# Two weight blocks at a time behind the normed tiles, and weight buffers released in halves, in a five-layer f32 kernel

## What is computed

```python
def rms_norm(x, g):
    xf = x.astype(jnp.float32)
    y = xf * lax.rsqrt(jnp.mean(xf * xf, axis=-1, keepdims=True) + EPS)
    return (y * g.astype(jnp.float32)).astype(x.dtype)
...
        idx_logits = jnp.einsum('bqhd,bsd->bqhs', qib.astype(jnp.float32), kf) * (IDX_HEAD_DIM ** -0.5)
        score = jnp.einsum('bqh,bqhs->bqs', wib.astype(jnp.float32) * (IDX_HEADS ** -0.5),
                           jax.nn.relu(idx_logits))
        adm = chunk_id[:, None, :] <= cqb[:, :, None]
        score = jnp.where(adm, score, -jnp.inf)
        top_val, top_idx = lax.top_k(score, k_sel)
```

## Time and profile before

| | |
|---|---|
| median of 3 runs | 1811.8 us (1811.22 to 1815.78) |
| profiled execution | 1814.44 us, of it the span 1812.4 us |
| mean granted clock of PE | 0.984 of full speed |
| PE, DVE, POOL, ACT busy | 95%, 69%, 45%, 44% of the span |
| matmuls | 13216 |
| HBM read | 150.5 MB, 84 GB/s over the span |

### The profile page before, as it was taken

How to read it: one execution, slowest core, us unless ns; L and a number is a source line. 1 busy time by engine, 2 the same in 40 slices (tenths; PEclk the granted TensorE clock), 3 DMA queues, 4 the chain that set the end, 5 groups by cost and what they waited for, 6 DMA issues and landing times.

```text
span 1812.4 us, 32762 instructions
## 1 busy us (share of the span) xinstructions
PE 1720.8 (95%) x13216; PEld 1285.5 (71%) x13216; DVE 1255.6 (69%) x2284; ACT 806.4 (44%) x1501; POOL 819.5 (45%) x721
## 2 busy tenths in 40 slices
PE   5999999999998989999999999899999999999997
PEld 5677777777776768667766666587677777777766
DVE  7599999999998676369975665545688517245553
ACT  3444534435433452465434443434576533344442
POOL 3544434444433255387851111444555555544433
PEclk9999999999999999999999999999999999999988
DMA  7222221222222132222221111132222232343312
GB/s 296 93 69 74 95 87 66 85 95 72 71 95 83 59 122 94 70 70 82 82 70 35 36 35 35 39 101 84 91 71 84 70 105 80 128 128 111 108 51 92
DMA packets 51877, 154.73 MB, mean 85 GB/s; under 512 B 5888, under 2 KB 12032, under 8 KB 51600
## 3 DMA queue, kind: packets, MB, share of 16 engines
q1 hardware_dynamic: 51728, 152.65, 25.1%
HBM read 150.50 MB, written 2.13 MB: 84 GB/s over the span
## 4 chain that ended last, share of the span: by engine, by line
PE 45%; DVE 11%; ACT 4%; issue 1%; POOL 1%; DVEq 0%; ACTq 0%; POOLq 0%
PE bank L509 10%; PE bank L505 10%; PE bank L506 10%; PE bank L2266 3%; PE bank L2254 3%; PE bank L2288 2%; DVE lru_xc L2708 2%; DVE score L2378 2%; DVE best L2375 2%; PE bank L2921 1%; PE bank L2936 1%; PE bank L548 1%; PE bank L550 1%; PE bank L549 1%; PE bank L2220 1%
## 5 line engine op out<-in xcount | busy, mean ns | idle before, releaser
L487 POOL TENSOR_TENSOR w_lo<-raw,w_hi 128x512 fp32r<-128x512 f32 (+2 forms) x434 | 582.7, 1363 | 651.5 <-ACT w_hi L469 651.1
L505 PE MATMUL bank<-h_hi,w_hi 128*128 128x512 f32 x1368 | 587.0, 429 | 24.4 <-ACT h_hi L949 10.2
L509 PE MATMUL bank<-h_lo,w_hi 128*128 128x512 f32 x1368 | 544.8, 398 | 10.1 <-DVE h_lo L923 5.7
L506 PE MATMUL bank<-h_hi,w_lo 128*128 128x512 f32 x1368 | 541.5, 396 | 0.0
L469 ACT ACTIVATE w_hi<-raw 128x512 fp32r<-128x512 f32 (+2 forms) x434 | 241.9, 601 | 279.8 <-PE bank L509 196.7
L505 PEld LDWEIGHTS bank<-h_hi,w_hi 128*128 128x128 f32 x1368 | 261.1, 191 | 113.0 <-issue 53.7
L509 PEld LDWEIGHTS bank<-h_lo,w_hi 128*128 128x128 f32 x1368 | 260.5, 190 | 79.9 <-DVE h_lo L923 10.5
L506 PEld LDWEIGHTS bank<-h_hi,w_lo 128*128 128x128 f32 x1368 | 261.9, 191 | 60.2 <-issue 13.9
L1553 DVE SCALAR_TENSOR_TENSOR ya<-padded,vecs,ya 128x512 f32<-128x512 f32 x240 | 216.3, 901 | 3.9
L2323 ACT ACTIVATE probs<-probs,small 128x512 f32<-128x512 f32 x64 | 46.3, 724 | 108.9 <-DVE small L2306 108.5
L2990 DVE CUSTOM_DVE_ANT_0 fox_probs<-bank,fox_keybias 128x128 f32<-128x128 f32 (+3 forms) x64 | 28.8, 488 | 85.0 <-PE bank L2921 84.7
(11 more groups left out here) (397 smaller groups left out, 2799.8 us busy)
## 6 DMA issues: line engine op xcount, KB each, us to landing
raw<-even_in SPq DMA_DIRECT2D x57, 512.0 KB, 3.8
raw<-odd_in SPq DMA_DIRECT2D x39, 512.0 KB, 3.4
raw<-ada SPq DMA_DIRECT2D x32, 512.0 KB, 4.1
raw<-fox_in SPq DMA_DIRECT2D x25, 512.0 KB, 3.6
raw<-lru_in SPq DMA_DIRECT2D x24, 512.0 KB, 3.4
ada_first<-ada SPq DMA_DIRECT2D x16, 512.0 KB, 14.0
raw<-even_out SPq DMA_DIRECT2D x16, 512.0 KB, 3.5
raw<-odd_out SPq DMA_DIRECT2D x16, 512.0 KB, 3.4
```

What stands on the lines that cost most here:

```text
L487: e.tensor_tensor(k.w_lo[s % NSPLIT][:, at], k.raw[n % NRAW][:, at], k.w_hi[s % NSPLIT][:, at].bitcast(F32), ALU.subtract).then_inc(*did(" ...
L505: e.matmul(out, hi[:, w], x[i][0], start=start and i == 0, stop=False, skip_group_check=True)
L506: e.matmul(out, lo[:, w], x[i][0], start=False, stop=False, skip_group_check=True)
L509: m = e.matmul(out, hi[:, w], x[i][1], start=False, stop=stop and i == kt - 1, skip_group_check=True)
```

## The change

1. `half_block`, `round_half`, `rest_half`, `project`, `project_values`: projecting a block now signals twice, after step 4 and after step 8, and the first half of block n+2 may be rounded after the first signal, if it fits in the first half of n.
2. Third layer: ki and qi0 are projected alternately, a step of each; what follows on ki moves to 1.9 (`main_end`), and the wi transposes from 1.0 to 1.7 behind qi0's number. DVE scales wi behind qi0's product instead of ahead of it.
3. Fourth layer: the steps of the first pair (lru 0 and gate 8) are mixed; `recurrence_times(0)` starts at 1.3 instead of 1.0, ACT's copy at 0.72, DVE's convolution at 0.77.
4. Fifth layer: fox_f's steps are put between value steps, and ACT rounds the next block ahead of the softplus.

```diff
@@ half_block
-    return n, key, slice(half * size, (half + 1) * size), k.plan[k.split[s - NSPLIT]][0] if s >= NSPLIT else None
+    old = None
+    if s >= NSPLIT:
+        old_key, _, old_kt, old_width, _ = k.plan[k.split[s - NSPLIT]]
+        soon = half == 0 and size <= old_kt // 2 * old_width
+        old = ("projected", old_key, old_kt // 2 - 1) if soon else ("projected", old_key)
+    return n, key, slice(half * size, (half + 1) * size), old
@@ project
         if i == kt - 1:
             m.then_inc(*did("projected", key))
+        elif i == kt // 2 - 1:
+            m.then_inc(*did("projected", key, i))
@@ main_times, main_end (third layer)
+    if key in INDEX[:2]:
+        return [block_number(INDEX[0]) + (2 * i + 0.5 + INDEX.index(key)) / DT for i in range(DT)]
     return [block_number(key) + (i + 0.5) / DT for i in range(DT)]
+def main_end(key):
+    return block_number(key) + (1.9 if key == INDEX[0] else 0.99)
@@ odd, PE
     def index_weights():
-        yield block_number(("qi", 0)) + 1.0
+        yield block_number(("qi", 0)) + 1.7
...
-    merge(main(), index_weights(), turn_values(), scores())
+    merge(main(INDEX[:1]), main(INDEX[1:] + MAIN), index_weights(), turn_values(), scores())
@@ odd, DVE; the same main_end on ACT and POOL
-            at = block_number(key) + 0.99
+            at = main_end(key)
...
-                if key == ("qi", 0):
+                if key == ("qi", 1):
                     ready(("multiplied", "wi_t"))
@@ lru
-    return spread_out(recurrence_labels(), n + 1.0, n + 1.9) if n + 1 < LT else spread_out(recurrence_labels(), 0.0, 1.6)
+    return spread_out(recurrence_labels(), n + (1.0 if n else 1.3), n + 1.9) if n + 1 < LT else spread_out(recurrence_labels(), 0.0, 1.6)
...
+        at = lru_times(0)
+        return (block(("lru", 0), ("activated", "lru_in", 0), [at[i] for i in (0, 2, 3, 5, 6, 8, 9, 11)]),
+                block(("lru", LT), ("made", "lru_gate", 0), [at[i] for i in (1, 4, 7, 10, 12, 13, 14, 15)]))
...
-            yield n + 0.55
+            yield n + (0.55 if n else 0.77)
...
-            yield n + 0.5
+            yield n + (0.5 if n else 0.72)
@@ fox
-    merge(block(("fox_f", 0), ("made", "fox_f"), [0.0] * DT))
...
+    merge(values(), block(("fox_f", 0), ("made", "fox_f"), [0.5, 1.5, 2.5, 3.1, 3.2, 3.3, 3.4, 3.5]))
...
+    round_ahead(k, e, need, did, k.nth["fox_f", 0] + NSPLIT)
     exp_of_minus_abs(e, need, did, "fox_softplus", k.rows[:, 0, :], k.rows[:, 1, :], ("made", "fox_f"))
-    round_ahead(k, e, need, did, k.nth["fox_f", 0] + NSPLIT)
```

More of the change, by code:

```diff
@@ L466, in round_half @@
     n, key, at, old = half_block(k, s, half)
-    for w in need((f"raw{n % NRAW}", key), old and ("projected", old)):
+    for w in need((f"raw{n % NRAW}", key), old):
         e.wait_ge(*w)
@@ L484, in rest_half @@
     n, key, at, old = half_block(k, s, half)
-    for w in need(("rounded", key, half), old and ("projected", old), (f"raw{n % NRAW}", key)):
+    for w in need(("rounded", key, half), old, (f"raw{n % NRAW}", key)):
         e.wait_ge(*w)
@@ L531, in project_tokens, with project_values @@
     m.then_inc(*did("projected", key))
-def project_values(k, e, need, did, name, part, taken, x_ready):
+def project_values(k, e, need, did, name, part, taken, x_ready, start):
     for b in range(TT):
@@ L545, in project_values @@
                 at = slice(tt * P, (tt + 1) * P)
+                yield start + ch * TT + tt
                 for v in need(("rest_made", key, i), ("rounded", key, i), *free, *x_ready(ch)):
@@ L550, in project_values @@
                 m = e.matmul(bank[:, :], k.H[ch][1][:, at], hi[:, w], start=False, stop=ch == DT - 1, skip_group_check=True)
-        m.then_inc(*did("projected", key))
+            m.then_inc(*(did("projected", key) if i == kt - 1 else did("projected", key, i)))
 def start_gpsimd(k, e):
@@ L2221, in scores, with main @@
                      skip_group_check=True).then_inc(*did("multiplied", "score", i))
-    def main():
-        for key in INDEX + MAIN:
+    def main(keys):
+        for key in keys:
             at = main_times(key)
@@ L2548, in main @@
         for key in INDEX + MAIN:
-            yield block_number(key) + 0.99
+            yield main_end(key)
             if key[0] in ("v", "g"):
@@ L2658, in blocks @@
     def blocks():
-        for n in range(LT):
+        for n in range(1, LT):
             at = lru_times(n)
@@ L2662, in blocks, with first_blocks @@
             yield from block(("lru", LT + n), ("made", "lru_gate", n), at[DT:])
+    def first_blocks():
+        at = lru_times(0)
+        return (block(("lru", 0), ("activated", "lru_in", 0), [at[i] for i in (0, 2, 3, 5, 6, 8, 9, 11)]),
+                block(("lru", LT), ("made", "lru_gate", 0), [at[i] for i in (1, 4, 7, 10, 12, 13, 14, 15)]))
     def recurrence(n):
@@ L2673, in recurrence @@
                      skip_group_check=True).then_inc(*did("multiplied", "lru_gates", n, i))
-    merge(blocks(), chain(*(recurrence(n) for n in range(LT - 1))))
+    merge(*first_blocks(), blocks(), chain(*(recurrence(n) for n in range(LT - 1))))
     k.end("tensor", "lru")
@@ L2901, in projections, with values @@
             yield from block((name, p), ("made" if name == "fox_g" else "activated", name, p), fox_times(name, p))
-    merge(block(("fox_f", 0), ("made", "fox_f"), [0.0] * DT))
-    for part in range(2):
-        taken = [k.work.take(value_done(part, tt)) for tt in range(TT)]
-        for tt, (bank, _) in enumerate(taken):
-            k.bank["fox_v", part, tt] = bank
-        project_values(k, e, need, did, "fox_v", part, taken, h)
+    def values():
+        for part in range(2):
+            taken = [k.work.take(value_done(part, tt)) for tt in range(TT)]
+            for tt, (bank, _) in enumerate(taken):
+                k.bank["fox_v", part, tt] = bank
+            yield from project_values(k, e, need, did, "fox_v", part, taken, h, part * DT * TT)
+    merge(values(), block(("fox_f", 0), ("made", "fox_f"), [0.5, 1.5, 2.5, 3.1, 3.2, 3.3, 3.4, 3.5]))
     merge(projections(0, 2))
```

## The result

| | before | changed |
|---|---|---|
| median | 1811.22 us (5 runs, 1808.49 to 1815.78) | 1819.96 us (5 runs, 1819.48 to 1821.64) |
| profiled execution, its span | 1814.44, 1812.4 us | 1819.48, 1817.8 us |
| ratio | | 1.0047, 95% interval 1.0031 to 1.0063 |

The changed kernel is slower by 8.5 us (0.0047 x 1811.2), between 5.6 and 11.4. The forecast was 1815.5, +3.7, in a range up to 1821.0: the side on which the sum came out was right and the range holds the time, but the size was less than half. The slower rival's 1818.9 is nearer to the 1820.0 measured than the forecast is. Profiled execution against profiled execution the difference is +5.0 us, nearer to the forecast, because that of before (1814.44) was one of its slower runs.

What follows compares the result with a forecast made beforehand. TensorE, busy 95% of the span, was taken as the bound, with a four-engine chain where the change reorders. Third layer +6.9, fourth -2.7, fifth -0.5, halves 0 gave +3.7 us on the median 1811.8: 1815.5, range 1807.5 to 1821.0.

Steps and rivals of the forecast that it cites:

- slower rival: Third layer: clock falls behind all three new holes, two more low stretches of 1.7 us; +7.1 us, 1818.9; chance 0.22.
- Step A: Third layer, ki and qi0 in pairs: the pair ends at 769.3 instead of 772.13, 2.8 us won; ki ends 2.1 later.
- Step B: Third layer, ahead of qi1: a new 4 us TensorE hole turns the 2.8 us won into a loss of 0.8.
- Step C: Third layer: transposes behind six steps of qi1 (4.1 us); swaps of qi0 and first score matmul 5.2 us late.
- low end: Third layer: TensorE's later idle time takes back at most 2.9 of the 5.2 us, leaving +2.3.
- Step D: Third layer: one low-clock stretch behind the first hole delays the transposes; +1.7 us, from none to three stretches (+5.1).
- Step E: Fourth layer: four more lru1 steps fill the 2.94 us idle ahead of the gates; -2.7 us, from -4.2 to -1.2.
- Step F: Fifth layer: value steps between fox_f's fill a 0.19 us wait and two short weight-load waits; -0.5 us, -1 to -0.2.
- step G: Halves, rounding half a block earlier: ScalarE's 196.7 us of waits mostly stay; 0 us, from -1 to +0.5.
- sign of being wrong: Halves: ScalarE's 196.7 us of waits cut by a third together with TensorE's idle time would break the claim of 0.

Runs made afterwards that it cites:

- e6: Changed kernel with the wi transposes ahead of qi1 again (1.7 back to 1.0), ki and qi0 still in pairs; 1.0004 of the kernel before.
- e9: Kernel before with only the wi transposes, and VectorE's scaling of wi, moved behind six steps of qi1, no pairing; 1.0020 of before.
- e7: Changed kernel with 18 spare matmuls, results unused, in the third layer's first hole, ahead of qi1; 1.0035 of the kernel before.
- e8: e7 with 12 more spare matmuls in the second hole, ahead of qi2; 1.0032 of the kernel before.
- e4: Kernel before with the halves alone: a weight buffer's first half given back after step 4, every order as before; 1.0001 of before.
- e10: e5 with 14 spare matmuls in the fourth layer's hole ahead of lru1; 0.9980 of the kernel before.
- e1: Kernel before with the third layer's part alone: ki and qi0 in pairs, wi transposes behind six steps of qi1; 1.0046 of before.
- e2: Kernel before with the fourth layer's part alone: the first pair's steps mixed, its recurrence placed later; 0.9986 of before.
- e5: Changed kernel with the third layer's part taken back; 0.9988 of the kernel before.
- e11: e6 with 14 spare matmuls in the hole ahead of the early transposes; 1.0008 of the kernel before.
- e3: Kernel before with the fifth layer's part alone: fox_f's steps between value steps, rounding ahead of the softplus; 1.0000 of before.

## Why the prediction was right in its side and short in its size

The forecast was +3.7 us with 0.60 on a change too small to be measured and 0.28 on a slower kernel; it is slower, clear of its interval. The mechanism of the loss was named, hole by hole. The time lies within the range because the range's top was drawn from the slower rival, and only one of that rival's two further low stretches is the change's doing. So the range held in part by luck.

**Step A** (2.8 us won at the pair's end). Measured 2.1: qi0 ends 13.1 us in instead of 15.2. The term took eight slow spacings from the start, and there were eleven and a shorter twelfth (the full pace is back at 762.33, 5.2 us in, not 3.6).

**Step B** (qi1 0.8 us later). The mechanism was right, down to POOL's w_lo as the releaser and a hole of 4.13 us where 4 were expected. qi1 starts 17.7 us in instead of 15.9, so 1.8 late where the term had 0.8. Of that 1.0 us, 0.8 comes from A's error: the last matmul of ki is 12.5 us in (769.62), not 11.7. The other 0.2 is the relay from there to qi1, 5.2 us instead of 5.0: POOL's w_lo follows ScalarE's rounding by 0.97 us (772.54 to 773.51), not by half a rounding, and the last leg is shorter. With the transposes put back, the pairing still costs 2.2 us to the first score (e6). This term was less than half of what it should have been.

**Step C** (transposes behind six steps, 4.1 us on the path to the score). Confirmed by itself: 4.0 us in e9. The idle time ahead of the swaps of qi0, 6.99 us, is the picture of it. The low end, that TensorE's later idle time gives some back, did not come: e9's layer is longer by the same 4.0 us (494.6 against 490.6), e6's by 2.3.

**Step D** (one low stretch, 1.7 us). One such stretch lies ahead of the transposes, and e7 prices it at 1.6 us. That there is one more was the slower rival's. The changed kernel's layer is 501.7 - 490.6 = 11.1 us over the undisturbed length, of which 8.0 are there at the first score. The next 1.5 us come right behind it. The second four score matmuls of the changed kernel:

```profile
793.77 1.13 PE L2236 MATMUL bank<-ki,qi 64*128 64x512 f32 x4
```

They start 4.23 us after the first four; before it was 2.66 (781.26 and 783.92). From there to the hole near 880 both kernels take 95.2 to 95.3 us. So the low stretch behind the second hole, which is free up to the score, costs 1.5 us behind it, and likewise 2.1 in e7 and, behind the third hole, 1.6 in e8. The last 1.6 us are not the change's: they come from a fall behind the hole ahead of 938.38, which stands in the kernel before as well and dropped the clock in e4 and e10 too, where nothing in this layer is new. From the hole near 880 to the next norm the changed kernel takes 369.9 us, e1, e4 and e10 370.0, and e2, e5, e6, e7, e9 and e11 368.3 to 368.4. So the slower rival was right in one of its two further stretches, 1.5 of its 3.4 us. The advice of the Trainium skill (TensorE: Matmul & The Clock Gate, section Why this matters for your kernels) against idle gaps between bursts of matmuls fits the first hole (4.13 us, 0.73 behind it). It is meant for long gaps, so the prediction stretched it when it counted the third hole (2.4 us as forecast, 1.19 measured), and the rows follow it in neither direction: the clock stayed at 1.00 behind 3.43 us of idle time in e8, and fell behind 2.05 us in the changed kernel.

Together, to the first score: 4.0 (e9) + 2.2 (e6) + 1.6 (e7) = 7.8, and the changed kernel has 8.0. The forecast had 5.2 + 1.7 = 6.9.

**Step E** (-2.7). One execution shows -3.4, the part alone -2.5, the traces at an equal clock -1.8 to -1.9 (e2). The hole of four steps closed as said and VectorE's chain moved up: the first pair's scan starts 20.5 us after the first lru_padded instead of 23.1. What was not counted is that the pairing makes the hole ahead of lru1 (3.43 us instead of 0.80), and where the clock falls behind it, the low stretch lies on lru1's steps. That costs 1.9 us of the layer's length, e5 against e8.

**Step F** (-0.5) and **step G** (0): no difference in the time that can be measured, as forecast (e3, e4). For F the traces have one: from the fifth layer's norm to the attention's last long hole 250.4 to 250.5 us in before, e1, e2 and e4, and 249.5 to 249.9 in e3, e5, e6, e7, e10 and e11. The changed kernel's own trace has 251.1, with a low clock of some 10 us from 1499 on, where before has some 7 us. G's reason is shown: a sixth of the 196.7 us went and no time with it. The sign of being wrong that I had named, a cut by a third together with TensorE's idle time, did not come.

The sum that the terms as measured would give is 8.0 + 1.5 - 1.9 - 0.6 + 0 = 7.0, where the timed difference is 8.5, from 5.6 to 11.4.

## What to carry to other kernels

Four small matmuls on an in-order queue cost nothing themselves, but all that waits for them pays for every instruction put ahead of them: ask of each moved step who is queued behind its result on the next engine. Pairing two blocks ends the pair earlier and the first of them later; if the buffers of the block behind the pair come free through a relay that starts with the first's end, what is won turns into a hole. A hole's low clock is worth mending only where the slow matmuls behind it stand on the path, and there a few spare matmuls do it.

## What was not expected of the hardware

The same holes make the clock fall in one execution and not in the next. In the kernel before, TensorE is idle for 2.42 us ahead of 921.76 and for 2.02 us ahead of 929.50, and the clock stays; in the changed kernel the holes are 2.40 us ahead of 930.64 and 2.05 ahead of 938.38, and it falls. Windows behind the second of them, before and then changed:

```profile
930.00:932.00 2.00, 2.00 (x10) 1.61 (x9) 0.00 (x0) 0.00 (x0) 1.24 (x1) 1.00 0.00 0
932.00:934.00 2.00, 2.00 (x11) 1.65 (x10) 0.00 (x0) 0.00 (x0) 0.00 (x0) 1.00 0.80 248
```

```profile
939.00:941.00 2.00, 2.00 (x8) 1.58 (x7) 0.00 (x0) 0.00 (x0) 1.08 (x1) 0.68 0.00 0
941.00:943.00 2.00, 2.00 (x6) 1.54 (x6) 0.00 (x0) 0.00 (x0) 0.00 (x0) 0.50 0.73 258
```

In the other traces of that unchanged stretch it falls behind one of the two holes in e1, e3, e4 and e10 and stays in e2, e5, e6, e7, e8, e9 and e11. Behind the hole of 1.6 us near 880 it falls in before and e8 alone. Without a fall the stretches agree closely: from the hole near 880 to the one near 922 it is 41.66 to 41.67 us in the changed kernel, e2 and e5, and 42.58 in before, where the clock fell behind the first. A fall does not always cost: in e3 the clock fell behind the hole near 921, and the layer still took 490.6 us. Where it does, it is 0.9 to 1.6 us a time. That this is a reason why runs of the kernel before spread over 1807 to 1816 us is likely but not shown. It is a warning against one profiled execution beside another: here they put the change at +5.0 where the timed runs say +8.5, and 2.3 us of the gap are in the table's last row, which the change does not touch.
